# Hybrid encoder layer: the ssm_b tables are issued later, and the last expert group's weights and v rows are handled in halves

## The reference

```
h = x + mixer_block(rms_norm(x))          # S5 state-space branch (tables b, c, lambda, dt) + latent attention, gated
h = h + memory_cross_attention(rms_norm(h), rms_norm(mem))
h = h + peer_ffn(rms_norm(h))             # product keys: 8 heads, top 16 of 16384 experts per token and head
out = rms_norm(h)

# s5_direction: ar, ai = exp(lam*dt);  bb = ((a - 1) / lam) * b        (32 groups, 64 states, 16 channels, 2 directions)
# peer_ffn, per token and head:
act = gelu(sum_d u_emb[idx] * x);  y += sum_k gate[k] * act[k] * v_emb[idx[k]]     # k over 16 experts
```

## Time and profile before

| | us |
|---|---|
| median of 3 runs | 2135.82 (2129.47 to 2137.36) |
| the profiled execution, its own time | 2135.21 |
| its span, first to last instruction | 2133.1 |

### The profile page before, as it was taken

The page is one execution under the profiler, slowest core; times in us unless marked ns, Lnnn a source line. Parts: engine busy times, 40 slices in busy tenths (PEclk is TensorE's granted clock), DMA queues, the critical chain, the costliest instruction groups (busy, mean ns, idle before and its releaser), DMA issues.

```text
span 2133.1 us, 19325 instructions
## 1 busy us (share of the span) xinstructions
PE 1786.3 (84%) x5959; PEld 974.6 (46%) x5959; DVE 1432.5 (67%) x2983; ACT 534.8 (25%) x1207; POOL 1168.6 (55%) x1171
## 2 busy tenths in 40 slices
PE   5988799999999969978788789878868977887687
PEld 5546434778997754423333233323323323332233
DVE  5598774444443488777777786687677777777763
ACT  3334443222333231212211221121112111311211
POOL 6990000000000077777777777777777777777773
PEclk9998899999999989999999889989989999999899
DMA  4211401334243099999999999999999999999996
GB/s 121 57 23 20 109 1 35 99 95 151 85 135 109 1 335 385 379 402 396 407 409 409 406 409 408 406 409 405 403 404 405 399 409 409 409 409 404 401 404 249
DMA packets 239390, 603.05 MB, mean 283 GB/s; under 512 B 38533, under 2 KB 105274, under 8 KB 239290
## 3 DMA queue, kind: packets, MB, share of 16 engines
q0 software_dynamic: 147840, 537.99, 64.0%
q1 hardware_dynamic: 91450, 63.85, 10.8%
HBM read 597.56 MB, written 2.10 MB: 281 GB/s over the span
## 4 chain that ended last, share of the span: by engine, by line
PE 39%; POOL 20%; DVE 15%; DMA 13%; issue 9%; ACT 3%; SPq 1%; DVEq 0%; ACTq 0%; POOLq 0%
PE bank L1562 19%; PE bank L1875 16%; POOL R L2002 13%; DMA R<-in_peer_v,R 4%; POOL WS L2002 3%; DMA WS<-in_peer_u,R 3%; DVE R L990 3%; PE bank L1853 3%; POOL slabs L2002 3%; DMA slabs<-in_peer_u,R 2%; DMA R<-in_peer_u,R 2%; DVE R L1449 1%; PE bank L1551 1%; DVE stat L1248 1%; DVE R L1403 1%
## 5 line engine op out<-in xcount | busy, mean ns | idle before, releaser
L1875 PE MATMUL bank<-R 128*128 128x512 f32 x2048 | 976.6, 627 | 231.6 <-ACT R L928 153.2
L1875 PEld LDWEIGHTS bank<-R 128*128 128x128 f32 x2048 | 391.9, 199 | 805.3 <-issue 600.1
L2002 POOL DMA_INDIRECT R<-in_peer_v,R x512 | 509.6, 995 | 162.2 <-issue 138.4
L2002 POOL DMA_INDIRECT WS<-in_peer_u,R x172 | 174.0, 1011 | 640.7 <-DVEq L1437 588.5
L1449 DVE CUSTOM_DVE_ANT_0 R<-WS,XN 128x1024 f32<-128x1024 f32 x172 | 210.7, 1225 | 98.7 <-DMA WS<-in_peer_u,R 93.5
L1449 DVE CUSTOM_DVE_ANT_0 R<-slabs,XN 128x1024 f32<-128x1024 f32 x168 | 205.8, 1225 | 98.6 <-DMA slabs<-in_peer_u,R 93.7
L1449 DVE CUSTOM_DVE_ANT_0 R<-R,XN 128x1024 f32<-128x1024 f32 x172 | 210.7, 1225 | 88.3 <-DMA R<-in_peer_u,R 82.8
L1562 PE MATMUL bank<-R 128*64 128x64 f32 (+6 forms) x792 | 193.7, 393 | 33.7 <-ACT R L708 11.6
L2002 POOL DMA_INDIRECT R<-in_peer_u,R x172 | 180.1, 1047 | 52.4 <-issue 52.4
L921 ACT ACTIVATE R<-R 128x16 f32<-128x16 f32 x32 | 6.9, 216 | 780.0 <-DVE R L1449 780.0
L2002 POOL DMA_INDIRECT slabs<-in_peer_u,R x168 | 169.9, 1011 | 56.5 <-issue 50.6
(11 more groups left out here) (215 smaller groups left out, 1914.0 us busy)
## 6 DMA issues: line engine op xcount, KB each, us to landing
slabs<-in_w_in SPq DMA_DIRECT2D x17, 512.0 KB, 5.3
slabs<-in_w_mem_kv SPq DMA_DIRECT2D x8, 1024.0 KB, 5.6
slabs<-in_w_peer_q SPq DMA_DIRECT2D x8, 1024.0 KB, 16.5
R<-in_peer_v,R POOLq DMA_INDIRECT x512, 12.3
slabs<-in_w_in SPq DMA_DIRECT2D x4, 1024.0 KB, 14.4
slabs<-in_w_ssm_glu SPq DMA_DIRECT2D x16, 256.0 KB, 3.1
slabs<-in_w_out SPq DMA_DIRECT2D x4, 1024.0 KB, 5.1
slabs<-in_w_mem_q SPq DMA_DIRECT2D x4, 1024.0 KB, 5.2
```

Of the source, the lines that this page charges most:

```text
L1875: last = pe.matmul(ps[2 * (t % 2) + n][:, :], diag[s % DRING], Vb[i % VRING][:, 512 * n:512 * n + 512], start=(s == 0), stop=(s == TOPK - 1))
L2002: pool.indirect_dma_start(out=dst, out_offset=None, in_=table, in_offset=bass.IndirectOffsetOnAxis(ap=ix[:, s:s + 1], axis=0)).then_inc(si ...
```

## The change

The ssm_b tables get a semaphore of their own, `d_ssb`. Their four DMAs are issued by POOL after its memsets and after slab `("u",1)` has landed. PE waits for the ssm_c tables alone. ACT takes one root of two values before it squares x. In the last group (g = 31) dot products, gelu, weights and diagonals come in two halves of eight slots, and v rows 0 to 7 of that group are gathered one by one behind v rows 8 to 15 of group 30. The orders in which PE takes slots and in which u rows are gathered are as before.

```diff
@@ ACT, the start
+            settle(act.activation(stat[0:G, 100:102], dtrow, ACT.Sqrt))
             squares(0, xn, FT[:, 0:2, :].rearrange("p k t -> p (k t)"))
@@ ACT, the expert stage
-            def gelu_of(g):
-                act.wait_ge(dots, (g + 1) * TOPK)
-                act.activation(gel, act_row, ACT.Gelu_apprx_tanh).then_inc(gelu_done, 1)
+            def gelu_of(g, part=slice(0, TOPK)):
+                act.wait_ge(dots, g * TOPK + part.stop)
+                act.activation(gel[:, part], act_row[:, part], ACT.Gelu_apprx_tanh).then_inc(gelu_done, 1)
-            def diagonals(g, t, first=False, slots=range(TOPK)):
-                act.wait_ge(w_ready, g + 1)
+            def diagonals(g, t, first=False, slots=range(TOPK), half=0):
+                act.wait_ge(w_ready, g + 1 + half)
@@ ACT, head(), last head
-                        diagonals(g, t)
+                        diagonals(g, t, slots=range(8))
+                        gelu_of(g, slice(8, TOPK))
+                        diagonals(g, t, slots=range(8, TOPK), half=1)
...
-                    if not last or t < NT - 1:
+                    if last and t == NT - 2:
+                        gelu_of(g + 1, slice(0, 8))
+                    elif not last or t < NT - 1:
                         gelu_of(g + 1)
@@ DVE, before the b tables are scaled
-            dve.wait_ge(d_ssm, 16 * 8)
+            dve.wait_ge(d_ssb, 16 * 4)
@@ DVE, head(), last head
+                    if last and t == NT - 2:
+                        for half, part in enumerate((slice(0, 8), slice(8, TOPK))):
+                            dot_products(g + 1, t + 1, range(part.start, part.stop))
+                            weights(g + 1, t + 1, part, half)
@@ PE, before the transposes of ssm_c
-            pe.wait_ge(d_ssm, 16 * 8)
+            pe.wait_ge(d_ssm, 16 * 4)
@@ POOL, the start: the four ssm_b DMAs move from in front of the memsets to here
             pool.sem_inc(zeros_set, 1)
+
+            await_slab(pool, ("u", 1))
+            for r, w in enumerate((ssm_b_re, ssm_b_im)):
+                for d in range(2):
+                    pool.dma_start(bb[r][64 * d:64 * d + 64, :, :],
+                                 w[0, d].rearrange("g p c -> p g c")).then_inc(d_ssb, 16)
 
             pool.wait_ge(trig_done, 3)
@@ POOL, head()
                         if more:
                             u_row(g + 1, (t + 1) % NT, s)
-                        v_row(g, t, s)
+                        if not last or t < NT - 1 or s >= 8:
+                            v_row(g, t, s)
+                        if last and t == NT - 2 and s >= 8:
+                            v_row(g + 1, t + 1, s - 8)
```

More of the change, by code:

```diff
@@ L346, in encoder_layer @@
         ld_v = [sem(f"ld_v{i}") for i in range(VRING)]
-        d_cst, d_vec, d_par, d_ssm = [sem(n) for n in ("d_cst", "d_vec", "d_par", "d_ssm")]
+        d_cst, d_vec, d_par, d_ssm, d_ssb = [sem(n) for n in ("d_cst", "d_vec", "d_par", "d_ssm", "d_ssb")]
         d_x = [sem(f"d_x{t}") for t in range(NT)]
@@ L1451, in dot_products, with weights @@
                     dve.wait_ge(dots, g * TOPK + (s + 1))
-            def weights(g, t):
-                dve.wait_ge(gelu_done, g + 1)
-                lstep(dve.tensor_tensor(wgt[t % 2], gel, gate[t % 2], ALU.mult))
+            def weights(g, t, part=slice(0, TOPK), half=0):
+                dve.wait_ge(gelu_done, g + 1 + half)
+                lstep(dve.tensor_tensor(wgt[t % 2][:, part], gel[:, part], gate[t % 2][:, part], ALU.mult))
                 dve.sem_inc(w_ready, 1)
@@ L1925, in _ @@
                                  w[0, d].rearrange("(b g) c p -> (g c) b p", b=NB)).then_inc(d_ssm, 16)
[L1926 to L1929, removed]
             step(pool.memset(mask, 1.0))
```

## The result

| | before | after |
|---|---|---|
| median of 20 runs, us | 2134.76 (2129.36 to 2139.65) | 2140.69 (2135.11 to 2148.98, and one of 2602.53) |
| ratio, 95% interval | | 1.0033 [1.0021, 1.0044] |
| profiled execution, its own time | 2135.21 | 2147.83 |

What follows compares the result with a forecast made beforehand. Bounds: at the start x's fourth tile, then POOL's chain; at the end v row 15 of group 30 landing plus 29.45 us of PE. 2135.2 - 5.0 + 8.9 = 2139.1, on the median 2139.7 us; range 2130 to 2148.

Steps and rivals of the forecast that it cites:

- The end, 8.9 us: Last two groups: seven more gathers of 1.27 us before v row 15 of group 30 lands; loses 8.9 us.
- Rival 2: Last groups: gathers don't hold back group 30's rows, so the tail costs nothing; 2130.8 us, chance 0.12.
- Rival 5: Last groups: TensorE's clock falls in PE's pauses, eight matmuls run more slowly, 2.5 us; 2142.2 us, chance 0.08.
- The b tables: Start: with b out of x's way, x lands at about 11.7 instead of 20.43 us, 8.7 earlier.
- rival 1: Start: b doesn't hold up x, so POOL's later issues put output_matrices(0) 3.8 us late; 2148.5 us, chance 0.10.
- the start's term: Start: output_matrices(0) begins at 58.0 instead of 62.99 us, a gain of 5.0 us.
- The root: Start, ACT: the early root removes the table load before L639, worth 1.0 us of path, not 1.28.
- POOL becomes the bound: Start: POOL's chain of 36.0 us from 22.0 ends at 58.0, later than DVE's 53.7, so gain 5.0, not 9.3.
- Rival 3: Start: POOL isn't the bound, its chain having fewer disturbances; gain up to 9.3 us, total 2135.4, chance 0.10.
- Rival 4: Start: POOL's issues of b are stretched beside DVE; gain only 1.2 us, total 2143.5, chance 0.10.
- The step that failed: Middle, between start and expert stage's end: no clock of its own, so the start's 5.0 us gain passes whole.
- the forecast's own signs of being wrong: Profile after: x still near 20 us, PE's last row shorter or earlier, or the middle not shifting with the start.

Runs made afterwards that it cites:

- The early root alone: Kernel before with only ACT's early root added, ssm_b as before; one run, 2134.08 us.
- the start alone: Kernel before plus only the change's start (ssm_b behind slab u1 with its own semaphore, early root), last group as before; 2277.96 against 2290.42 us, ratio 0.9992.
- the kernel with small products: The start alone, with PE's small transpose of the gain vectors done 24 times instead of once; 2130.84 us, ratio 0.9974 to the kernel before.
- b on SP's queue: As the start alone, but SP issues the four ssm_b DMAs behind the third slab, POOL none; 2289.30 us, ratio 0.9998 to the kernel before.
- both together: Kernel before plus the start of b without the wait, halves, and group 30's v rows all gathered before group 31's; 2125.49 against 2136.19 us, ratio 0.9950.
- b without the wait: As the start alone, but POOL issues ssm_b right after its memsets, not waiting for slab u1; 2286.40 us, ratio 0.9907 to the kernel before.
- the start repeated: The kernel of the start alone timed again on a quiet occasion; 2132.99 against 2136.26 us for the kernel before, ratio 0.9985.

## Why the prediction came out as it did

**The end, 8.9 us: right.** Measured 77.33 - 68.46 = 8.87, and 77.35 - 68.58 = 8.77 in the pair of one set. The mechanism is the one named: seven more gathers of 1.27 us ahead of the landing that PE needs. POOL's first early issue waited 3.97 us for slot 4, and the landings went on every 1.26 us, so the wait cost nothing. It did use up part of the reserve: that gather, issued at 2071.92, landed at 2081.88, the median from issue to landing was 9.0 us instead of 13.0, and for 2 us few new transfers began (columns as the earlier trace rows):

```profile
2072.00:2074.00 2.00, 1.79 (x4) 0.68 (x4) 0.74 (x3) 0.00 (x0) 1.70 (x2) 1.00 0.28 74
```

PE's last row began 12.6 us later than in before's trace and not about 4: 8.9 are the tail's, and the other 3.8 were there at slot 0 of group 30 already, in this long execution and with the start's gain missing.

Rival 2 (a tail at no cost) is out. Rival 5 didn't happen: the clock stayed at 1.00 over the pauses of 1.8 us; the 68 matmuls again took 29.45.

**The b tables: right, with a late slab.** x landed at 12.4 (forecast 11.7), 8.0 us earlier. In all 14 traces it is 12.4 to 13.3 with b issued later and 19.2 to 21.6 with b issued first, so rival 1 is out. The Trainium skill, in "DMA: Bandwidth & Descriptors", section "Queues, rings and completion order", has each DMA engine take turns between the queue rows that have work. The trace agrees: with no b beside x the DMAs moved 339 to 373 GB/s between 8 and 16 us, where before they moved 117 to 150 between 10 and 18. Slab u1 landed at 18.74 instead of 17.5, and POOL's copy came at 23.35 instead of 22.0. That 1.35, less 0.2 by which the rest of the chain was shorter than its 36.0 + 33.1 = 69.1 us before, is the 5.0 - 3.84 = 1.16 by which the start's term was too large.

**The root: right.** The early root alone shows 1.0 us.

**POOL becomes the bound: right, and its chain was mis-sized twice.** I took 36.0 us from before for POOL's first copy to output_matrices(0); it took 64.48 - 23.35 = 41.1, and output_matrices(0) started at 64.48 and not at 58. DVE's `negC` came 14.7 us earlier than before and not 9.3, as DVE's chain also got faster: the 14 operations of 128x32 ahead of it took 6.88 us instead of 11.57. So DVE's long two-input operations fell beside POOL's table levels and no longer beside the outputs. Stretches of after (us, busy of PE, PEld, DVE, ACT, POOL, clock, DMA share, GB/s):

```profile
47.00:57.00 10.00, 9.11 (x50) 8.84 (x49) 9.38 (x7) 2.15 (x6) 9.48 (x7) 1.00 0.16 41
57.00:64.00 7.00, 7.00 (x28) 3.92 (x27) 0.00 (x0) 4.69 (x13) 6.53 (x7) 1.00 1.00 215
```

With DVE busy for 9.38 of 10 us POOL needs 1.49 for 256 elements, where before, beside small operations of DVE, it needed 0.68. With DVE idle it needs 1.05 for 512 elements, where before it needed 1.39, and 1.10 for the first one of outputs(0), where before it was 2.08. The levels lost 5.1 us and the outputs gained 5.3. Copy to `table_done` is 92.25 - 23.35 = 68.90, against 96.09 - 26.56 = 69.53. The total moved by 0.6, of which 0.43 is the idle gap that I had counted.

The split is steady: 41.1 and 27.8 us in all four traces with the wait for the slab, 36.0 to 37.4 and 33.0 to 33.1 in the ten others. Rival 3, "fewer disturbances", is wrong: they moved. Rival 4 is out: the four issues took 1.09 each, not more. (Its remark that DVE worked little while b was issued before is too strong: DVE was busy for 1.35 of the 2 us from 6 to 8.) The Trainium skill, in "SBUF — State Buffer", section "Who interferes with whom", calls the port pair that DVE and GpSimd share the only point of contention and an exclusive lock. The two directions of the rows agree with it: 0.68 became 1.49, and 2.08 became 1.10.

**The step that failed: "What lies between starts when its predecessor ends and has no clock of its own, so a shift of the start should go through it whole".** That the middle doesn't shift with the start was one of the forecast's own signs of being wrong, and it came. Of the 3.84 us at `table_done` the trace keeps nothing: the first gather is 0.66 later. Over the six traces with before's start and the four with the change's, `table_done` is at 95.97 and 92.59 on average, and the first gather at 747.95 and 748.70. PE's matmul no. 750 starts 3.0 us earlier than before, no. 850 1.4, no. 1000 0.3, and no. 1100 1.4 later. The same 100 matmuls from no. 750 on take 12.72 us before and 14.3 after. Stretches there (columns as above), of before:

```profile
182.00:186.00 4.00, 4.00 (x21) 1.80 (x19) 3.83 (x6) 0.06 (x1) 0.00 (x0) 1.00 0.75 87
186.00:190.00 4.00, 1.77 (x9) 0.69 (x8) 2.25 (x4) 1.46 (x3) 0.00 (x0) 1.00 0.16 18
190.00:194.00 4.00, 4.00 (x70) 3.81 (x69) 0.33 (x1) 3.74 (x12) 0.00 (x0) 1.00 0.02 4
```

of after:

```profile
182.00:186.00 4.00, 1.77 (x9) 0.69 (x8) 3.17 (x5) 1.46 (x3) 0.00 (x0) 0.97 0.32 38
186.00:190.00 4.00, 4.00 (x31) 2.30 (x30) 0.00 (x0) 1.56 (x6) 0.00 (x0) 0.60 0.00 0
190.00:194.00 4.00, 4.00 (x61) 3.93 (x58) 1.58 (x3) 4.00 (x11) 0.00 (x0) 1.00 0.02 4
```

Both have the same pause, 1.77 busy of 4 us. Before, the clock is 1.00 after it; after the change it falls: 0.60 is the mean of a stretch mostly at the lower level (0.50, 1.2 GHz), and PE is busy for all 4 us with 31 matmuls. From 70 to 260 us the clock was at 0.50 for 41 us before and for 61 us after.

This low stretch, 3.4 us at 0.50 beginning between 180 and 187 us, is there in six of the 14 traces: after, the start alone and its repeat, the kernel with small products, b on SP's queue and both together. It is in none that keeps before's start; there the 100 matmuls take 12.7. Between `table_done` and the first gather the six take 655.1 to 656.6 us and the other eight 651.0 to 653.3, so the two groups are 4.0 us apart on average. Between 70 and 260 us the clock was at 0.50 for 47.8 to 61.4 us in the six and for 37.5 to 44.4 in the eight. The 100 matmuls show 1.6 of the 4.0; that the clock takes the rest is likely but not shown.

It isn't the shift alone that brings the stretch: b without the wait had no such stretch (12.72 us) and kept its gain in full at the first gather (748.08 - 738.07 = 10.0, of 9.0 at `table_done`), and both together, with the same code in its start, had one (14.3) and kept 4.1 of 7.8:

```profile
182.00:186.00 4.00, 4.00 (x61) 3.93 (x60) 1.44 (x3) 4.00 (x12) 0.00 (x0) 1.00 0.01 4
186.00:190.00 4.00, 4.00 (x35) 3.83 (x35) 3.75 (x5) 1.95 (x3) 0.00 (x0) 1.00 0.00 0
```

(b without the wait), and

```profile
178.00:182.00 4.00, 1.77 (x7) 0.52 (x5) 2.69 (x4) 1.46 (x3) 0.00 (x0) 0.84 0.22 27
182.00:186.00 4.00, 4.00 (x43) 2.44 (x42) 0.00 (x0) 1.71 (x6) 0.00 (x0) 0.73 0.00 0
```

(both together). What sets it off stays open; the attempt to move it by earlier work failed.

How much of the start's gain arrives on average is open as well. The traces say that nothing arrives; the timings of the start repeated say that 3.2 us (0.9 to 5.8) arrive at the end. Single traces can't settle that: before's own kind of start had its first gather between 746.29 and 749.43, and from the first gather to the end the four quiet traces with before's tail take 1381.6 to 1385.0.

The forecast of 2139.7 against 2140.69 is so a right end of 8.9 and a start that was forecast at 5.0, was 3.8 at `table_done`, and by the change's timing is worth 8.9 - 5.9 = 3.0. That it came within 1 us is partly luck: it forecast a difference of 3.9 where 5.9 was measured, and its base, the median of three runs, lay 1.1 above the median of twenty.

## What to carry to other kernels

When two chains meet, work out for each what it waits for and then what it runs *beside*. Pulling one ahead can move a mutual slowdown from one part of the other to another, with a sum near zero. Where a stage ends on work that runs in a fixed order, gathers are worth ordering by when that work needs them: with the halves, the same gathers gave +8.9 us in one order and -3.3 in another, by the traces. And a wait put in front of DMA issues on an engine with a long chain of its own is paid by that chain: here 5 us for a slab that had 7 us of slack.

## Of the hardware, not expected

- A pause of TensorE of the same form (1.77 us busy in 4) was followed by a granted clock of 1.00 in before's trace, and by 3.4 us at 0.50 in six traces whose `table_done` lay 3.3 to 8.1 us earlier. Of two runs with the same code in the start only one had it. It is worth 1.6 us in 100 matmuls.
- POOL and DVE slow each other. On POOL a two-input operation of 256 elements took 0.68 us beside DVE's small operations and 1.49 beside its long ones. On DVE `negC`, with one input, took 1.38 us beside POOL's operations of 512 and 0.52 beside those of 128.
- Issues of b's tables took 1.09 us each whether POOL issued them at 10 or at 19 us, while DVE was busy for 1.8 or for 0.8 of 2 us.
- Gathers of 512 KB on POOL's queue landed some 1.26 us apart whether they had been issued 13 or 9 us before, and through a pause of 4 us in issuing.
